# Compressing the keys and values of a sparse-attention layer over 128 partitions instead of twice 64

## The chip, the cores and the metric

One NeuronCore of a Trainium2 chip runs the whole program. The metric is the device time of one execution in microseconds; lower is better. Before the change it is 853.73 us (median of three runs, 852.6 to 855.01). The profile shown below is of one further execution, which took 855.14 us; what the profiler saw of it, the span, is 853.4 us.

## The reference, cut to what matters

The program computes one layer of a hybrid decoder for a prompt of 512 tokens and 8 single-token samples with 256 cached tokens each. One of its four mixers is native sparse attention (NSA). Its compressed branch makes one key and one value for each block of 32 tokens, every 16 tokens, by a linear map of the raw rows of the block (64 numbers a token, for each of 2 heads `kv`):

```python
# phi: (2, 32 * 64, 64), one map for keys (comp 0) and one for values (comp 1)
# raw rows of one sequence: kc_raw, vc_raw of (tokens, 2 heads, 64)
# block n covers tokens 16 n ... 16 n + 31
kc = blocks(kc_raw).reshape(n, 2, 32 * 64) @ phi[0] + phi_b[0]     # then RMS norm
vc = blocks(vc_raw).reshape(n, 2, 32 * 64) @ phi[1] + phi_b[1]
```

A block is two neighbouring chunks of 16 tokens. The kernel therefore multiplies each chunk once by the first half of phi and once by the second, and adds the second product of chunk n+1 to the first product of chunk n. There are 32 chunks of the prompt and 8 times 16 of the samples, 160 in all (`N_CHUNK`).

The rest of the layer matters here only for what stands before and behind: norms and the input projection before, the other mixers, the attention proper, the output projection and a mixture of 32 experts behind.

## The kernel before, in words

All orders are written out by hand: each engine has one block of code, and engines meet at semaphores. PSUM has 8 banks; `psum_jobs()` gives every product a job name and a bank, six of them in rotation. `claim` waits on TensorE until the bank's previous job has been read, `filled` tells the readers, `taken` waits for that, `copied` frees the bank, and `drained` waits until it is free (lines 440 to 456). All matrix data here is fp32. `mm` (line 1110) is a matmul and `turn` (line 1113) a transpose through TensorE, which is why nearly all TensorE rows of the profile name one of these two lines.

The stages that matter, in TensorE's order:

1. Input projection of 5 tiles of tokens (lines 1200 to 1221). Behind the matmuls of each tile TensorE transposes q, k of the tile before (`K` jobs) and its raw compressed rows (`R` jobs). Between the tiles stand the samples: `sample_keys(b)` (line 1182) transposes the cached raw rows of sample b into job `sR{b}` (4 transposes of 128 by 128) and its other keys into `sK{b}` (4 more), and then adds `sample_scores(b - 1)`, two matmuls with 32 output rows. Sample 0 stands in the tile after the first two, 1 and 2 in the next, 3 to 5 in the last, 6 and 7 at the end.
2. Between samples 5 and 6 stands job `RS`, whose product VectorE uses in one long instruction (line 1671) that scales the transposed activations; until that is done the bank of `RS` is not free, and the job that claims it next is `sK7`.
3. The compression (lines 1234 to 1243). ScalarE has copied all `R` and `sR` jobs into `raw`, laid out as partition = 64 kv + d, then component, then token, so one place j of all 160 chunks is every sixteenth number. For each component and each of the 16 places there are two matmuls, kv = 0 on partitions 0 to 63 and kv = 1 on 64 to 127, with 128 output rows (both halves of phi) and 160 columns, each kv into its own bank.
4. ScalarE and VectorE add the two halves (lines 878 to 883 and 1679 to 1685), and TensorE goes on with the other projections in feature-major form (`features`, line 1244), 32 matmuls of 260 columns for each group.

Much later come the attention, the output projection, and then the experts: SyncE's queue loads 32 experts of 6 MB each into three buffers, and the load of expert e starts when TensorE is done with the same part of expert e-3 (lines 580 to 606).

Of the kernel before, what the change touches and what calls it, by code (L numbers as in the profile page):

```python
# [18 lines left out]
ALU = mybir.AluOpType  # L19
ACT = mybir.ActivationFunctionType  # L20
# [3 lines left out]
SEQ = 512  # L24
# [44 lines left out]
def psum_jobs():  # L69

    jobs, turn = [], [0]

    def take(name, bank=None):
        if bank is None:
            bank = turn[0] % 6
            turn[0] += 1
        jobs.append((name, bank))

    def feature(g, halves=(0, 1)):
        for j in halves:  # L80
            take(f"F{g}{j}0")
            take(f"F{g}{j}1")

    take("gain")
    for i in range(4):
        take(f"xTa{i}")
        take(f"xTb{i}")
    take("xT4")
    last = None
    for i in PROJ_TILES:  # L90
        take(f"A{i}")
        if i < 4:
# [12 lines left out]
        last = i  # L105
    take("RS")
    take("K3")
    take("R3")
    for b in SAMPLES_AT["end"]:
        take(f"sR{b}")  # L110
        take(f"sK{b}")
    take("SS", 6)
    take("SW", 7)
    for n in ("CK0", "CK1", "CV0", "CV1"):
        take(n)
# [60 lines left out]
    take("posB")  # L176
    take(f"hTb{others[-1]}")
    take("posC")
    take("cnt", 6)
    return jobs  # L180


def layer_kernel(nc, a, o):
# [7 lines left out]
    with ctx:  # L191
# [45 lines left out]
        ynsa = reg_h.cut(1280, "p (t f) -> p t f", t=5)  # L237
        qT = reg_q.cut(2 * T, "p (g t) -> p g t", g=2)
        kT = reg_q.cut(2 * T, "p (r t) -> p r t", r=2)
        raw = reg_x.t[:, :].rearrange("p (c t) -> p c t", c=2)  # L240
        gain_rows = reg_y.cut(128)[0:KC]
        root_diag = reg_y.cut(512, "p (t n) -> p t n", t=4)
        par_rows = reg_y.cut(128)[0:P_ROWS]
# [5 lines left out]

        phi = reg_a.cut(4096, "p (c j h n) -> p c j h n", c=2, j=16, h=2)
        page_k = [reg_a.cut(768, "p (g f) -> p g f", g=2) for _ in range(PAGE_BUFS // 2)]
        win_k = [reg_a.cut(256, "p (g f) -> p g f", g=2) for _ in range(PAGE_BUFS // 2)]
        vs_cache = reg_a.cut(2048, "p (b g f) -> p b g f", b=NS, g=2)
# [196 lines left out]
        def copied(ins, job):  # L452
            ins.then_inc(bank_read[bank_of[job]], 1)
# [37 lines left out]
        def _(sp_eng):  # L491
# [24 lines left out]
            eng.dma_start(kg[:, :, :], a["nsa_qk_g"].rearrange("l r d -> (l r) d")[2:4].partition_broadcast(128)).then_inc(S["kg_loaded"], 16)  # L516
            eng.dma_start(pages[:, :], a["page_table"].rearrange("b n -> (b n)").unsqueeze(0)).then_inc(S["pages_loaded"], 16)
            for c in range(2):
                for kv in range(2):
                    for half in range(2):  # L520
                        src = a["nsa_phi"].rearrange("l c (h j d) n -> d (l c h) j n", h=2, d=HD)[:, 2 * c + half]
                        eng.dma_start(phi[64 * kv:64 * kv + 64, c, :, kv ^ half, :], src).then_inc(S["phi_loaded"], 16)
            eng.wait_ge(S["blocks_zeroed"], 1)

            for k in range(4):
# [6 lines left out]
            for b in range(NS):  # L532
                k = b % PAGE_BUFS
                if b >= PAGE_BUFS:
                    eng.wait_ge(bank_full[bank_of[f"sK{b - PAGE_BUFS}"]], turn_of[f"sK{b - PAGE_BUFS}"] + 1)
                for g in range(2):
                    page = eng.value_load(pages[0:1, 2 * b + g:2 * b + g + 1], min_val=0, max_val=cache.shape[0] // PAGE - 1)
                    rows_of_page = cache[bass.ds(page * PAGE, PAGE)]
                    eng.dma_start(page_k[k][:, g, :], rows_of_page[:, 0:384]).then_inc(smp_loaded[k], 16)
                    eng.dma_start(vs_cache[:, b, g, :], rows_of_page[:, 384:512]).then_inc(S["vcache_loaded"], 16)  # L540
# [248 lines left out]
        def _(eng):  # L789
# [43 lines left out]
            def feature_qk(i):  # L833

                r, c = ROWS[i], COL[i]
                ps = taken(eng, f"K{i}")
                if i == 4:
                    eng.wait_ge(S["params_made"], 1)
                v = ps[:, 0:4 * r].rearrange("p (g t) -> p g t", g=4)
                eng.activation(qT[:, :, c:c + r], v[:, 0:2, :], ACT.Copy, scale=qg_scaled)  # L840
                copied(copy(kT[:, :, c:c + r], v[:, 2:4, :]), f"K{i}")
                if i < 4:
                    ps = taken(eng, f"R{i}")
                    copied(copy(raw[:, :, c:c + r], ps[:, 0:256].rearrange("p (g t) -> p g t", g=2)), f"R{i}")

            def sample_keys(b):

                ps = taken(eng, f"sR{b}")
                copied(copy(raw[:, :, SEQ + PAST * b:SEQ + PAST * (b + 1)], ps[:, :].rearrange("p (c t) -> p c t", c=2)), f"sR{b}")
                if b >= 2:  # L850
                    eng.wait_ge(S["sample_scores"], b - 1)
                if b == 0:
# [23 lines left out]
                sample_keys(b)  # L876

            for comp, (name, out) in enumerate((("CK", kc_a), ("CV", vcT))):
                for kv in range(2):
                    lo = 64 * kv  # L880
                    other = 64 - lo
                    ps = taken(eng, f"{name}{kv}")
                    eng.activation(out[lo:lo + 64, 0:N_CHUNK - 1], ps[other:other + 64, 1:N_CHUNK], ACT.Identity, bias=params[lo:lo + 64, P_PHI_B + comp:P_PHI_B + comp + 1]).then_inc(S["kc_copied"], 1)
# [224 lines left out]
        def _(eng):  # L1108
# [73 lines left out]
            def sample_keys(b):  # L1182
                eng.wait_ge(smp_loaded[b % PAGE_BUFS], 48 * (b // PAGE_BUFS + 1))
                ps = claim(eng, f"sR{b}")
                for c in range(2):
                    for g in range(2):
                        ins = turn(ps[:, 256 * c + 128 * g:256 * c + 128 * g + 128], page_k[b % PAGE_BUFS][:, g, 128 * c:128 * c + 128])
                filled(ins, f"sR{b}")
                ps = claim(eng, f"sK{b}")
                for g in range(2):  # L1190
# [41 lines left out]
            eng.wait_ge(S["phi_loaded"], 16 * 8)  # L1232
            drained(eng, f"sR{NS - 1}")
            for comp, name in enumerate(("CK", "CV")):
                ps2 = [claim(eng, f"{name}{kv}") for kv in range(2)]
                for j in range(16):
                    for kv in range(2):

                        lo = 64 * kv
                        src = raw[lo:lo + 64, comp, :].rearrange("p (n s) -> p n s", s=16)[:, :, j]  # L1240
                        ins = mm(ps2[kv][:, 0:N_CHUNK], phi[lo:lo + 64, comp, j].rearrange("p h n -> p (h n)"), src, j == 0, j == 15)
                        if j == 15:
                            filled(ins, f"{name}{kv}")
# [326 lines left out]
        def _(eng):  # L1570
# [106 lines left out]
            eng.memset(kcT[:, N_CHUNK - 1:N_CHUNK], 0.0)  # L1677
            eng.memset(vcT[:, N_CHUNK - 1:N_CHUNK], 0.0)
            for comp, (name, first, out) in enumerate((("CK", kc_a, kcT), ("CV", vcT, vcT))):
                for kv in range(2):  # L1680
                    lo = 64 * kv
                    eng.wait_ge(S["kc_copied"], 2 * comp + kv + 1)
                    ps = taken(eng, f"{name}{kv}")
                    copied(tt(out[lo:lo + 64, 0:N_CHUNK - 1], first[lo:lo + 64, 0:N_CHUNK - 1], ps[lo:lo + 64, 0:N_CHUNK - 1], ALU.add), f"{name}{kv}")
                    drained(eng, f"{name}{kv}")
                if comp == 0:
                    eng.sem_inc(S["kc_sum"], 1)
            drained(eng, "CN")
# [473 lines left out]
```

## Time and profile before

| what | value |
|---|---|
| median of 3 runs | 853.73 us |
| profiled execution, its time | 855.14 us |
| profiled execution, its span | 853.4 us |
| TensorE (PE) busy | 730.8 us, 86% |
| VectorE (DVE) busy | 202.8 us, 24% |
| ScalarE (ACT) busy | 148.8 us, 17% |
| GpSimd (POOL) busy | 182.2 us, 21% |
| read from and written to device memory | 264.87 MB |
| compression on TensorE | 95.89 to 113.43 us |

PE stands for matmuls and PEld for the weight loads that run beside them. One fp32 matmul of the code leaves two records of each kind in the trace, a transpose leaves one. A shape such as `64*128 64x160` says 64 rows and 128 columns of weights and a moving operand of 64 partitions by 160 numbers. `SPq` is time in which SyncE issues transfers. A busy time of a merged row overlaps the next row a little, since the end of a matmul record lies behind the start of the next; so lengths are best taken from start to start.

### The profile page before, as it was taken

The page shows a single profiled execution, that of the slowest core. Times are in us where ns is not written, and L with a number is a line of the kernel's source. Part 1 is how long each engine was busy: PE and PEld are TensorE (multiplying, and loading weights), DVE is VectorE, ACT ScalarE, POOL GpSimd, SP SyncE. Part 2 cuts the span into 40 slices and gives each one's busy share as a digit, 9 for nine tenths or more (in the row PEclk, how much of TensorE's full clock was granted, in tenths as well). Part 3 has the DMA queues.
Part 4 walks back from the last instruction along what each step waited for, and adds up shares of the span by engine and source line. Part 5 has one row for each costly group of instructions (what it writes and reads, how often), then busy time and mean ns, then how long its engine had stood idle before and what let it go on. Part 6 is the DMA issues. An engine that isn't in the chain of part 4 may idle for free.

```text
span 853.4 us, 10234 instructions
## 1 busy us (share of the span) xinstructions
PE 730.8 (86%) x3647; PEld 378.4 (44%) x3647; DVE 202.8 (24%) x575; ACT 148.8 (17%) x363; POOL 182.2 (21%) x188
## 2 busy tenths in 40 slices
PE   6999999999989999599999997877777777777783
PEld 5788688777767445333333332222222222222220
DVE  2422303636687112711011100100100100101120
ACT  5223313015544312110100100000000000000000
POOL 5010000061100000113323332132132132132121
PEclk9999999999998999789999999999999999999997
DMA  9652924020800794569999999999999999999992
GB/s 301 121 154 62 278 105 107 2 75 1 296 2 1 282 422 189 198 243 409 410 412 408 408 412 404 418 412 408 413 415 407 415 413 409 416 415 408 416 413 74
DMA packets 76885, 246.52 MB, mean 289 GB/s; under 512 B 24944, under 2 KB 44303, under 8 KB 52235
## 3 DMA queue, kind: packets, MB, share of 16 engines
q1 hardware_dynamic: 63697, 230.96, 68.4%
q0 software_dynamic: 11776, 8.58, 4.6%
q10 hardware_dynamic: 1378, 6.54, 1.9%
q8 instruction: 19, 0.31, 0.1%
q14 instruction: 15, 0.12, 0.0%
HBM read 239.95 MB, written 24.92 MB: 310 GB/s over the span
## 4 chain that ended last, share of the span: by engine, by line
PE 49%; SPq 33%; DMA 6%; DVE 5%; issue 3%; ACT 1%; POOL 1%; ACTq 0%; POOLq 0%; DVEq 0%
PE bank L1110 47%; SPq L588 23%; SPq L595 10%; DMA reg_b<-in_exp_w_gu 3%; PE bank L1113 3%; DMA reg_w<-in_w_in 1%; DMA ffn_in<-reg_x 1%; DVE reg_y L2106 1%; DVE reg_a L1896 1%; ACT reg_y L1093 1%; DVE reg_y L2114 1%; DVE reg_b L1671 1%; DVE small L1856 1%; POOL small L693 0%; DVE reg_y L1903 0%
## 5 line engine op out<-in xcount | busy, mean ns | idle before, releaser
L1110 PE MATMUL bank<-reg_w,reg_y 128*64 128x512 f32 (+2 forms) x512 | 137.0, 573 | 15.6 <-DMA reg_w<-in_exp_w_gu 15.6
L1110 PE MATMUL bank<-reg_a,reg_y 128*64 128x512 f32 x528 | 124.2, 607 | 22.3 <-DMA reg_a<-in_exp_w_gu 16.6
L1110 PE MATMUL bank<-reg_b,reg_y 128*64 128x512 f32 x528 | 122.8, 600 | 22.3 <-DMA reg_b<-in_exp_w_gu 16.6
L2110 DVE TENSOR_TENSOR reg_y<-reg_y,bank 128x256 f32<-128x256 f32 x32 | 13.5, 422 | 418.7 <-ACT reg_y L1093 418.7
L1110 PEld LDWEIGHTS bank<-reg_w,reg_y 128*64 128x64 f32 (+2 forms) x512 | 45.4, 144 | 95.2 <-issue 54.0
L1110 PE MATMUL bank<-reg_b,reg_w 128*128 128x260 f32 x384 | 85.6, 384 | 0.0
L1110 PEld LDWEIGHTS bank<-reg_a,reg_y 128*64 128x64 f32 x528 | 34.6, 138 | 103.3 <-issue 50.5
L1110 PEld LDWEIGHTS bank<-reg_b,reg_y 128*64 128x64 f32 x528 | 34.6, 136 | 101.3 <-issue 58.1
L1110 PEld LDWEIGHTS bank<-reg_b,reg_w 128*128 128x128 f32 x384 | 72.7, 190 | 12.1 <-issue 1.3
L1113 PE MATMUL bank<-small,reg_y 128*128 128x128 f32 (+3 forms) x206 | 42.8, 317 | 24.7 <-DVE reg_y L2110 15.0
L1110 PE MATMUL bank<-reg_w,reg_b 128*128 128x256 f32 (+2 forms) x320 | 62.2, 389 | 1.2 <-DMA reg_w<-in_w_in 1.2
L763 POOL DMA_INDIRECT out_y_p<-reg_y,reg_h x16 | 25.3, 1583 | 168.5 <-ACT reg_y L1097 160.3
L1093 ACT ACTIVATE reg_y<-bank,small 128x256 f32<-128x256 f32 x32 | 15.2, 473 | 264.0 <-PE bank L1110 264.0
L763 POOL DMA_INDIRECT out_y_p<-reg_h x16 | 25.3, 1579 | 160.9 <-issue 160.9
L693 POOL TENSOR_TENSOR small<-small 128x1 f32<-128x1 f32 (+4 forms) x18 | 15.8, 896 | 192.6 <-DVE small L1945 69.8
L1110 PEld LDWEIGHTS bank<-reg_w,reg_b 128*128 128x128 f32 (+1 forms) x320 | 52.1, 174 | 10.0 <-issue 1.3
L1113 PEld LDWEIGHTS bank<-small,reg_y 128*128 128x128 f32 (+3 forms) x206 | 29.6, 202 | 57.4 <-issue 35.4
L1110 PE MATMUL bank<-reg_h,reg_y 128*64 128x512 f32 x160 | 36.6, 600 | 5.2 <-DVE reg_y L2114 5.2
L758 POOL DMA_INDIRECT reg_y<-ffn_in,reg_h x32 | 35.0, 1095 | 21.2 <-issue 19.0
L1113 PE MATMUL bank<-small,reg_b 128*128 128x128 f32 (+2 forms) x133 | 21.3, 284 | 6.8 <-ACT reg_b L976 3.6
L1097 ACT ACTIVATE reg_y<-bank,small 128x512 f32<-128x512 f32 x16 | 11.0, 687 | 87.3 <-PE bank L1110 87.3
L763 POOL DMA_INDIRECT out_y_s<-reg_y,reg_h x16 | 24.9, 1554 | 4.9 <-issue 4.9
(357 smaller groups left out, 632.8 us busy)
## 6 DMA issues: line engine op xcount, KB each, us to landing
reg_a<-in_exp_w_gu SPq DMA_DIRECT2D x44, 1024.0 KB, 27.9
reg_b<-in_exp_w_gu SPq DMA_DIRECT2D x44, 1024.0 KB, 27.6
reg_w<-in_exp_w_gu SPq DMA_DIRECT2D x40, 1024.0 KB, 28.0
reg_a<-in_exp_w_down SPq DMA_DIRECT2D x22, 1024.0 KB, 28.3
reg_b<-in_exp_w_down SPq DMA_DIRECT2D x22, 1024.0 KB, 28.2
reg_h<-in_exp_w_down SPq DMA_DIRECT2D x20, 1024.0 KB, 28.2
reg_w<-in_w_in SPq DMA_DIRECT2D x9, 1024.0 KB, 10.9
reg_w<-in_w_out SPq DMA_DIRECT2D x2, 2048.0 KB, 11.0
```

The costliest lines, as they stand in the source:

```text
L588: eng.dma_start(gu_w[g][:, lo:lo + width, :], src).then_inc(gu_loaded[g][part], 16)
L595: eng.dma_start(down_w[g][:, half], src).then_inc(down_loaded[g][half], 16)
L693: eng.tensor_tensor(out, in_, minus_half[0:out.shape[0], 0:out.shape[-1]], ALU.pow).then_inc(S[s_done], 1)
L758: eng.indirect_dma_start(xe_rows[e % 2], None, x1_dram, idx, bounds_check=2 * T - 1, oob_is_err=False).then_inc(x_gathered[e % 2], 16)
L763: eng.indirect_dma_start(y, idx, y_out[e % 2], None, bounds_check=last, oob_is_err=False, compute_op=ALU.add).then_inc(y_scattered[e % 2], 16)
L1093: eng.activation(silu[b], bank[2 + b][:, 0:256], ACT.Silu, scale=slot_scale[:, 1, bass.ds(e, 1)]).then_inc(S["silu_done"], 1)
L1097: eng.activation(y_out[b], bank[6 + b][:, :], ACT.Copy, scale=slot_scale[:, 0, bass.ds(e, 1)]).then_inc(S["y_copied"], 1)
L1110: return eng.matmul(out, lhsT, rhs, start=start, stop=stop, skip_group_check=True)
L1113: return eng.transpose(out, in_, ident[0:in_.shape[0], 0:in_.shape[0]])
L1671: copied(tt(xnT[:, :, 0:SEQ], xnT[:, :, 0:SEQ], ps[:, :].unsqueeze(1).to_broadcast([128, KC, SEQ]), ALU.mult), "RS")
L1856: eng.tensor_reduce(att_mx[:, col:col + 1], ps[:, 0:width], X_AXIS, ALU.max, negate=True).then_inc(S["att_max"], 1)
L2110: tt(hid[b], silu[b], bank[2 + b][:, 256:512], ALU.mult).then_inc(S["hid_made"], 1)
```

## The change

`raw` is laid out by place within the chunk. A pair of neighbouring tokens lies one above the other: partition = 64 * (token odd) + d, then component, kv, pair j (8 of them), chunk n. With that one place pair of all chunks and both heads is a contiguous piece of 160 numbers for each head, and one matmul over 128 partitions takes 2 times 160 columns. Phi is laid out the same way and takes half the room.

```diff
-        raw = reg_x.t[:, :].rearrange("p (c t) -> p c t", c=2)
+        raw = reg_x.t[:, :].rearrange("p (c k j n) -> p c k j n", c=2, k=2, j=8)
-        phi = reg_a.cut(4096, "p (c j h n) -> p c j h n", c=2, j=16, h=2)
+        phi = reg_a.cut(2048, "p (c j h n) -> p c j h n", c=2, j=8, h=2)
+        reg_a.at = 4096
 # SyncE: phi, 8 transfers of 128 KB in place of 8 of 256 KB
-                        eng.dma_start(phi[64 * kv:64 * kv + 64, c, :, kv ^ half, :], src)
+                        eng.dma_start(phi[64 * odd:64 * odd + 64, c, :, half, :], src)
 # SyncE: a page of 128 tokens onto 64 partitions, two tokens each
-                    eng.dma_start(page_k[k][:, g, :], rows_of_page[:, 0:384])
-                    eng.dma_start(vs_cache[:, b, g, :], rows_of_page[:, 384:512])
+                    pairs = rows_of_page.rearrange("(m o) f -> m o f", o=2)
+                    eng.dma_start(page_k[k][64 * g:64 * g + 64, :, :], pairs[:, :, 0:384])
+                    eng.dma_start(vs_cache[64 * g:64 * g + 64, b, :, :], pairs[:, :, 384:512])
 # ScalarE: job R of a tile, four copies in place of one
-                    copied(copy(raw[:, :, c:c + r], ps[:, 0:256].rearrange("p (g t) -> p g t", g=2)), f"R{i}")
+                    for kv in range(2):
+                        by_pair = ps[64 * kv:64 * kv + 64, 0:256].rearrange("p (c n j o) -> p c n j o", c=2, j=8, o=2)
+                        for odd in range(2):
+                            ins = copy(raw[64 * odd:64 * odd + 64, :, kv, :, c // 16:c // 16 + 8].rearrange("p c j n -> p c n j"), by_pair[:, :, :, :, odd])
+                    copied(ins, f"R{i}")
 # ScalarE: job sR, one copy as before, with a step of 160 numbers in what it writes
-                copied(copy(raw[:, :, SEQ + PAST * b:SEQ + PAST * (b + 1)], ps[:, :].rearrange("p (c t) -> p c t", c=2)), f"sR{b}")
+                copied(copy(raw[:, :, :, :, first:first + N_CMP_S].rearrange("p c k j n -> p (c k) n j"), ps[:, :].rearrange("p (x n j) -> p x n j", x=4, j=8)), f"sR{b}")
 # TensorE: job sR, eight matmuls by the identity in place of four transposes
-                    for g in range(2):
-                        ins = turn(ps[:, 256 * c + 128 * g:256 * c + 128 * g + 128], page_k[b % PAGE_BUFS][:, g, 128 * c:128 * c + 128])
+                    for kv in range(2):
+                        at = 128 * c + 64 * kv
+                        for odd in range(2):
+                            ins = mm(ps[64 * odd:64 * odd + 64, 2 * at:2 * at + 128], page_k[b % PAGE_BUFS][:, odd, at:at + 64], ident, True, True)
 # TensorE: the compression
-                ps2 = [claim(eng, f"{name}{kv}") for kv in range(2)]
-                for j in range(16):
-                    for kv in range(2):
-                        lo = 64 * kv
-                        src = raw[lo:lo + 64, comp, :].rearrange("p (n s) -> p n s", s=16)[:, :, j]
-                        ins = mm(ps2[kv][:, 0:N_CHUNK], phi[lo:lo + 64, comp, j].rearrange("p h n -> p (h n)"), src, j == 0, j == 15)
+                ps = claim(eng, name)
+                for j in range(8):
+                    ins = mm(ps[:, 0:2 * N_CHUNK].rearrange("p (k n) -> p k n", k=2), phi[:, comp, j].rearrange("p h n -> p (h n)"), raw[:, comp, :, j, :], j == 0, j == 7)
+                filled(ins, name)
 # the jobs CK0, CK1, CV0, CV1 (four banks) become CK and CV (two banks); ScalarE and VectorE
 # read the same four pieces of 64 x 159 numbers as before, from two banks
```

Two places of TensorE's order show the change. The first is sample 1, behind the projection of its tile (the third of five); `bank` is PSUM, `small` holds the identity, `reg_a` and `reg_b` hold the cached rows, `reg_h` the rows of the prompt. Before:

```order
L1110 MATMUL bank<-reg_w,reg_b 128x268 x8
L1113 MATMUL bank<-small,reg_b 128x128 x2
L1113 MATMUL bank<-small,reg_h 128x128 x4
L1113 MATMUL bank<-small,reg_a 128x128 x8
L1110 MATMUL bank<-reg_a,reg_b 32x257 x2
```

and now:

```order
L1118 MATMUL bank<-reg_w,reg_b 128x268 x8
L1121 MATMUL bank<-small,reg_b 128x128 x2
L1121 MATMUL bank<-small,reg_h 128x128 x4
L1118 MATMUL bank<-small,reg_a 64x128 x8
L1121 MATMUL bank<-small,reg_a 128x128 x4
L1118 MATMUL bank<-reg_a,reg_b 32x257 x2
```

Of the eight transposes of a sample four remain; the other four have become eight matmuls with 64 output rows, and TensorE goes through one more kind of output shape per sample. The second place is the end of the samples and the compression (`reg_x` is `raw`). Before:

```order
L1113 MATMUL bank<-small,reg_b 128x128 x8
L1110 MATMUL bank<-reg_a,reg_b 32x257 x4
L1110 MATMUL bank<-reg_x,reg_a 128x160 x64
L1110 MATMUL bank<-reg_b,reg_w 128x260 x32
L1110 MATMUL bank<-reg_b,small 128x160
```

and now:

```order
L1118 MATMUL bank<-small,reg_b 64x128 x8
L1121 MATMUL bank<-small,reg_b 128x128 x4
L1118 MATMUL bank<-reg_a,reg_b 32x257 x4
L1118 MATMUL bank<-reg_x,reg_a 128x320 x16
L1118 MATMUL bank<-reg_b,reg_w 128x260 x32
L1118 MATMUL bank<-reg_b,small 128x160
```

The 64 matmuls of 160 columns have become 16 of 320; what stands behind them is the same.

## Rows read from the trace of the kernel before

**Rows 1.** The page's chain of work that ended last, by engine.

```profile
PE 49%; SPq 33%; DMA 6%; DVE 5%; issue 3%; ACT 1%; POOL 1%; ACTq 0%; POOLq 0%; DVEq 0%
```

**Rows 2.** Stretches: length, busy time per engine, clock, DMA share, GB/s.

```profile
365.00:503.00 138.00, 128.07 (x588) 46.76 (x586) 16.14 (x34) 13.36 (x22) 43.22 (x31) 0.98 0.98 389
503.00:833.00 330.00, 261.83 (x1132) 80.21 (x1131) 32.49 (x72) 23.90 (x41) 86.37 (x61) 1.00 1.02 412
```

**Rows 3.** SyncE in order of time: start, length, what; first load into a used buffer.

```profile
370.13 5.47 SPq L588 DMA_DIRECT2D reg_a<-in_exp_w_gu  x4
```

**Rows 4.** TensorE in order of time: the compression and the first features.

```profile
95.89 17.61 PE L1110 MATMUL bank<-reg_x,reg_a 64*128 64x160 f32 x128
113.43 14.29 PE L1110 MATMUL bank<-reg_b,reg_w 128*128 128x260 f32 x64
```

**Rows 5.** TensorE in order of time, samples 1 and 2.

```profile
65.79 1.04 PE L1113 MATMUL bank<-small,reg_a 128*128 128x128 f32 x8
66.75 0.63 PE L1110 MATMUL bank<-reg_a,reg_b 128*32 128x257 f32 x4
67.31 1.09 PE L1113 MATMUL bank<-small,reg_b 128*128 128x128 f32 x8
68.33 0.63 PE L1110 MATMUL bank<-reg_a,reg_b 128*32 128x257 f32 x4
```

**Rows 6.** TensorE in order of time, RS to the last sample.

```profile
88.31 1.16 PE L1110 MATMUL bank<-reg_y,small 128*128 128x128 f32 x8
89.31 0.38 PE L1113 MATMUL bank<-small,reg_b 128*128 128x128 f32 x2
...
91.49 0.66 PE L1113 MATMUL bank<-small,reg_b 128*128 128x128 f32 x4
93.99 0.66 PE L1113 MATMUL bank<-small,reg_b 128*128 128x128 f32 x4 [1.84 <-DVE reg_b L1671]
94.58 1.38 PE L1110 MATMUL bank<-reg_a,reg_b 128*32 128x257 f32 x8
```

**Rows 7.** VectorE in order of time: the scaling that reads RS.

```profile
89.51 4.42 DVE L1671 TENSOR_TENSOR reg_b<-reg_b,bank 128x4096 f32<-128x4096 f32 x1 [0.69 <-PE bank L1110]
```

**Rows 8.** TensorE, matmuls with few output rows, at three places.

```profile
30.16 3.80 PE L1110 MATMUL bank<-reg_w,reg_b 128*8 128x256 f32 x64
...
161.39 3.61 PE L1110 MATMUL bank<-reg_a,reg_b 128*32 128x128 f32 x64 [1.63 <-DVE reg_b L1765]
164.93 0.41 PE L1110 MATMUL bank<-reg_h,reg_b 8*32 8x128 f32 x4
...
380.63 7.04 PE L1110 MATMUL bank<-reg_b,reg_y 128*64 128x512 f32 x32
```

**Rows 9.** TensorE, attention scores over 64 partitions, 256 and 384 columns.

```profile
222.48 0.70 PE L1110 MATMUL bank<-reg_q 64*128 64x256 f32 x4
223.12 0.29 PE L1110 MATMUL bank<-causal_bf,ident_bf 128*128 128x128 bf16 x2
...
236.46 0.92 PE L1110 MATMUL bank<-reg_q 64*128 64x384 f32 x4
237.31 0.29 PE L1110 MATMUL bank<-causal_bf,ident_bf 128*128 128x128 bf16 x2
```

**Rows 10.** ScalarE in order of time, copies of jobs K2, R2 and sR4.

```profile
84.05 0.39 ACT L792 ACTIVATE reg_q<-bank 128x256 f32<-128x256 f32 x1
84.31 0.89 ACT L792 ACTIVATE reg_x<-bank 128x256 f32<-128x256 f32 x2
...
85.84 0.60 ACT L792 ACTIVATE reg_x<-bank 128x512 f32<-128x512 f32 x1
86.34 0.20 ACT L792 ACTIVATE reg_a<-reg_q 128x2 f32<-128x2 f32 x1
```

**Rows 11.** SyncE's queue: the loads of weights for the features.

```profile
89.68 52.74 SPq L550 DMA_DIRECT2D reg_w<-in_w_in  x6
```

**Rows 12.** Stretches: length, clock, DMA share, GB/s.

```profile
104.00:106.00 2.00, 1.00 0.98 307
106.00:108.00 2.00, 1.00 0.06 20
```

More of the change, by code:

```diff
@@ L113, in psum_jobs @@
     take("SW", 7)
-    for n in ("CK0", "CK1", "CV0", "CV1"):
-        take(n)
+    take("CK")
+    take("CV")
     feature("U")
@@ L518, in _ @@
             for c in range(2):
-                for kv in range(2):
+                for odd in range(2):
                     for half in range(2):
-                        src = a["nsa_phi"].rearrange("l c (h j d) n -> d (l c h) j n", h=2, d=HD)[:, 2 * c + half]
-                        eng.dma_start(phi[64 * kv:64 * kv + 64, c, :, kv ^ half, :], src).then_inc(S["phi_loaded"], 16)
+                        src = a["nsa_phi"][0, c].rearrange("(h j o d) n -> h o d j n", h=2, o=2, d=HD)[half, odd]
+                        eng.dma_start(phi[64 * odd:64 * odd + 64, c, :, half, :], src).then_inc(S["phi_loaded"], 16)
             eng.wait_ge(S["blocks_zeroed"], 1)
@@ L538, in _ @@
                     rows_of_page = cache[bass.ds(page * PAGE, PAGE)]
-                    eng.dma_start(page_k[k][:, g, :], rows_of_page[:, 0:384]).then_inc(smp_loaded[k], 16)
-                    eng.dma_start(vs_cache[:, b, g, :], rows_of_page[:, 384:512]).then_inc(S["vcache_loaded"], 16)
+                    pairs = rows_of_page.rearrange("(m o) f -> m o f", o=2)
+                    eng.dma_start(page_k[k][64 * g:64 * g + 64, :, :], pairs[:, :, 0:384]).then_inc(smp_loaded[k], 16)
+                    eng.dma_start(vs_cache[64 * g:64 * g + 64, b, :, :], pairs[:, :, 384:512]).then_inc(S["vcache_loaded"], 16)
                 eng.dma_start(win_k[k][:, :, :], win_state[b].rearrange("(g p) f -> p g f", p=128)[:, :, 0:128]).then_inc(smp_loaded[k], 16)
@@ L843, in feature_qk @@
                     ps = taken(eng, f"R{i}")
-                    copied(copy(raw[:, :, c:c + r], ps[:, 0:256].rearrange("p (g t) -> p g t", g=2)), f"R{i}")
+                    for kv in range(2):
[3 more added lines that the diff above has]
+                    copied(ins, f"R{i}")
             def sample_keys(b):
                 ps = taken(eng, f"sR{b}")
-                copied(copy(raw[:, :, SEQ + PAST * b:SEQ + PAST * (b + 1)], ps[:, :].rearrange("p (c t) -> p c t", c=2)), f"sR{b}")
+                first = N_CMP_P + N_CMP_S * b
+                copied(copy(raw[:, :, :, :, first:first + N_CMP_S].rearrange("p c k j n -> p (c k) n j"), ps[:, :].rearrange("p (x n j) -> p x n j", x=4, j=8)), f"sR{b}")
                 if b >= 2:
@@ L878, in _ @@
             for comp, (name, out) in enumerate((("CK", kc_a), ("CV", vcT))):
+                ps = taken(eng, name)
                 for kv in range(2):
@@ L881, in _ @@
                     other = 64 - lo
-                    ps = taken(eng, f"{name}{kv}")
-                    eng.activation(out[lo:lo + 64, 0:N_CHUNK - 1], ps[other:other + 64, 1:N_CHUNK], ACT.Identity, bias=params[lo:lo + 64, P_PHI_B + comp:P_PHI_B + comp + 1]).then_inc(S["kc_copied"], 1)
+                    first = N_CHUNK * kv + 1 - kv
+                    eng.activation(out[lo:lo + 64, 0:N_CHUNK - 1], ps[other:other + 64, first:first + N_CHUNK - 1], ACT.Identity, bias=params[lo:lo + 64, P_PHI_B + comp:P_PHI_B + comp + 1]).then_inc(S["kc_copied"], 1)
             eng.wait_ge(S["kc_sum"], 1)
@@ L1185, in sample_keys @@
                 for c in range(2):
-                    for g in range(2):
-                        ins = turn(ps[:, 256 * c + 128 * g:256 * c + 128 * g + 128], page_k[b % PAGE_BUFS][:, g, 128 * c:128 * c + 128])
+                    for kv in range(2):
+                        at = 128 * c + 64 * kv
+                        for odd in range(2):
+                            ins = mm(ps[64 * odd:64 * odd + 64, 2 * at:2 * at + 128], page_k[b % PAGE_BUFS][:, odd, at:at + 64], ident, True, True)
                 filled(ins, f"sR{b}")
@@ L1234, in _ @@
             for comp, name in enumerate(("CK", "CV")):
-                ps2 = [claim(eng, f"{name}{kv}") for kv in range(2)]
-                for j in range(16):
-                    for kv in range(2):
-                        lo = 64 * kv
-                        src = raw[lo:lo + 64, comp, :].rearrange("p (n s) -> p n s", s=16)[:, :, j]
-                        ins = mm(ps2[kv][:, 0:N_CHUNK], phi[lo:lo + 64, comp, j].rearrange("p h n -> p (h n)"), src, j == 0, j == 15)
-                        if j == 15:
-                            filled(ins, f"{name}{kv}")
+                ps = claim(eng, name)
+                for j in range(8):
+                    ins = mm(ps[:, 0:2 * N_CHUNK].rearrange("p (k n) -> p k n", k=2), phi[:, comp, j].rearrange("p h n -> p (h n)"), raw[:, comp, :, j, :], j == 0, j == 7)
+                filled(ins, name)
             def features(g, halves_of=(0, 1)):
@@ L1679, in _ @@
             for comp, (name, first, out) in enumerate((("CK", kc_a, kcT), ("CV", vcT, vcT))):
+                eng.wait_ge(S["kc_copied"], 2 * comp + 2)
+                ps = taken(eng, name)
                 for kv in range(2):
[L1681 to L1685, printed above, removed]
+                    lo, at = 64 * kv, (N_CHUNK + 1) * kv
+                    ins = tt(out[lo:lo + 64, 0:N_CHUNK - 1], first[lo:lo + 64, 0:N_CHUNK - 1], ps[lo:lo + 64, at:at + N_CHUNK - 1], ALU.add)
+                copied(ins, name)
+                drained(eng, name)
                 if comp == 0:
```

## The prediction, on record before the result

> **What bounds the kernel now.** I read the chain of waits first: TensorE holds 49% of it and SyncE's issuing 33% [rows 1]. So there are two regimes, and the stretches show where they meet [rows 2]: from 365 to 503 us TensorE is busy 128 of 138 us, from 503 to 833 us only 262 of 330 while the DMA engines are full at 412 GB/s. A change at 30 to 113 us can move the end only if the DMA-bound part starts earlier with it. It does: the first load into a buffer that was already used starts at 370.13 us, when TensorE has finished that part of the first expert [rows 3], and the chain in front of it is TensorE nearly throughout. So I carry one microsecond of TensorE's path before 113 us to the end as one microsecond. A cold clock at the first expert can add or take about a microsecond of that at random.
>
> Second, TensorE in order of time around the edit. The compression runs from 95.89 to 113.43 us, 17.54 us, with no idle time before or behind it [rows 4]. The samples are 1.52 us each (65.79 to 67.31 us) with no idle time either [rows 5]. Only at the end does TensorE wait: 1.84 us before the last four transposes [rows 6], for the VectorE instruction that starts when RS is filled and lasts 4.42 us [rows 7].
>
> **The compression: what it costs and why.** 64 pairs of records in 17.54 us are 0.274 us a pair. Are the two members of a pair, on partitions 0 to 63 and 64 to 127, really serial? The attention scores use the same two halves with contiguous operands: four records of 256 columns take 0.64 us to the next kind, four of 384 take 0.85 [rows 9]. 128 more columns cost 0.21 us for four records; that is two rounds of 0.107, so the two halves run side by side, at 0.83 ns a column. In the compression a pair of 160 columns at this rate would be 0.133 us. It is twice that. What differs is the operand: every sixteenth number. So I read the half rate as the price of the step, and the merging of the two halves as worth nothing in itself.
>
> The Trainium skill says the same of both: in "TensorE: Matmul & The Clock Gate", part 3, matmuls on different row groups run concurrently, and "SBUF — State Buffer", in the section on door 1, says that accesses which cross to a new 16-byte line each time pay a penalty. By the first rule alone a change from 64 to 128 partitions saves nothing; by the second the contiguous layout is what saves. The trace agrees with the first (0.21 us above) and is consistent with the second (0.274 against 0.133 us).
>
> After: 16 matmuls are 32 records of 320 contiguous columns. The features give the price, 14.29 us for 64 records of 260 columns [rows 4], 0.223 us or 0.858 ns a column; 320 columns are 0.275 us and 32 of them 8.8 us. Saved: 17.54 - 8.8 = 8.7 us, and one change of tile shape (64 to 128 rows) at its exit, 0.15 us by the price below. Together -8.9 us. Bounds: at 0.83 ns a column 8.5 us are left (-9.2); if columns of `raw` kept today's 1.71 ns, 17.5 us (no gain).
>
> **The samples: what is added on TensorE.** Four transposes of each sR become eight matmuls, 16 records, that alternate between output rows 0 to 63 and 64 to 127. Prices from rows: eight transposes take 0.96 us before a new shape when they follow other transposes and 1.02 when they follow a different shape [rows 5]; four take 0.59 (93.99 to 94.58) [rows 6]. So a transpose is 0.108 us and a change of shape 0.09 + 0.06 = 0.15 us.
>
> The alternating pair isn't in the trace at 128 columns. Lower bound: with 8 output rows, four column groups and 256 columns, 64 records take 3.80 us, 0.238 a round of four [rows 8], and experts' pairs of 64 output rows take 7.04 us for 32 records of 512 columns, 0.44 a pair [rows 8]. A quarter of that is 0.11 us for a pair of 128 columns. Upper bound: four groups of 32 output rows at 128 columns take 161.39 to 164.93 us for 64 records, 0.22 a round [rows 8], twice the streaming time of 0.107; so a round with many short loads can cost double. I take 0.112, since this row has four weight loads a round and the new code two, and the experts' row has the same tile shape.
>
> A sample then adds 8 x 0.112 - 4 x 0.108 + 0.15 (a second change of shape) = 0.62 us. Samples 0, 1, 3 and 6 follow transposes, where no change of shape was needed before: 0.15 more each. On the path, samples 0 to 5: 6 x 0.62 + 3 x 0.15 = 4.2 us. Upper bound, with 0.22: 8 x 0.22 - 0.43 + 0.15 = 1.48, so 9.3 us; lower, with the changes of shape hidden, 6 x 0.45 = 2.7 us.
>
> "TensorEngine Tiling (Array Packing)" of the Trainium skill says in its key properties that changing the tiling mode drains the engine, and in its gotchas that column tiling excludes the fp32 transpose mode, which is why matmuls stand here. It speaks against this change; the trace shows the drain at 0.15 us.
>
> Samples 6 and 7 add 2 x 0.62 + 0.15 = 1.4 us between RS and sK7. There TensorE waits 1.84 us for VectorE, whose 4.42 us run from RS and not from the samples. The addition disappears in the wait: cost 0, and 1.3 us with the upper bound (3.1 - 1.84).
>
> **What lies beside.** ScalarE: each R job becomes four copies. A copy of 256 columns starts 0.26 us after the one before it and one of 512 takes 0.50 [rows 10], so four of 128 are some 0.6 to 0.7 us, 0.4 more, in front of the copies of the samples. TensorE needs a sample's sK copy one sample later (now 2.1 us), and ScalarE's work for one is 0.50 + 0.10 + 0.50 = 1.1 us. This covers the four copies, and a strided write of sR up to three times as slow (1.5 + 0.1 + 0.5 = 2.1). Cost 0; at four times as slow about 3.5 us, 3.0 of it the two copies of sR6 and sR7 at 2.0 in place of 0.5 us in front of the last scores. Phi's loads halve, in front of the pages, which can only arrive earlier: 0. The feature weights are issued from 89.68 us [rows 11], behind page loads that wait for sK3, and all four land by 106 us [rows 12]. Both move: sK3 is filled about 2.9 us later, so the last lands near 109 us, and the first of the four, the only one needed then, well before; the features start at 95.89 + 4.2 + 8.8 = 108.9 us. ScalarE and VectorE read CK and CV from two banks, 14 us ahead of the product that needs them: 0.
>
> **The sum.** -8.9 + 4.2 + 0 = -4.7 us. The profiled execution took 855.14 us (span 853.4), so the changed kernel under the same conditions takes 850.4; the median of before is 853.73, 1.4 lower, and from it I get 849.0 us.
>
> **The rivals.**
> 1. Double rounds: the pairs of sR cost 0.22 us, as the row with 32 output rows does. For it: that row is the only one with 128 columns in column groups. Against it: it has twice the groups. Then +9.3 + 1.3 - 8.9 = +1.7 us, 855.4.
> 2. Slower: the alternating output halves don't overlap and each weight load is exposed. 16 records of 0.108 + 0.06 us are 2.7 us in place of 0.43, and with the change of shape 2.4 us a sample: 6 x 2.4 + 0.45 = 14.9, samples 6 and 7 exceed the wait by 3.1, so -8.9 + 18.0 = +9.1 us, 862.8. Against it stands the experts' pair. It breaks even at a round of 0.19 us and is slower by over 2.6 us from 0.23 on.
> 3. The change doesn't do what it says: the half rate is not the step's but the operand's or the tile's, and 320 columns cost 0.55 us. Then no gain, +4.2 us, 857.9. The features and the experts read at full rate from the same kind of memory, against it.
> 4. ScalarE's strided writes are four times as slow: -4.7 + 3.5, 852.5.
>
> **How the numbers follow.** Forecast (a round up to 0.14 us) 65%, 849.0 with its own range 846.8 to 851; rival 1 and rounds between 17%; rival 2 7%; rival 3 4%; rival 4 or another partial loss 7%. A difference under 0.3%, 2.6 us, can't be told from none. The low end is the lower bound of the samples, -6.2, and a run 0.7 below it: 846.8. The high end reaches into rival 1 until a fifth at most is left out: 854.2. Faster 0.69, same 0.21, slower 0.10.
>
> **What would show it.** In the changed profile: 32 records of 128x320 in 8.8 us; each sR 16 records in 0.9 to 1.0 us (1.8 with rival 1, 2.7 with rival 2); the wait of 1.84 us before the last transposes down to about 0.4; features from 109 us; the first reused expert buffer loaded from about 365.5 us. I am wrong if the 16 records of an sR take more than 1.5 us, if the 320 columns take more than 0.4 us, or if a wait for a DMA stands in front of the features.

## The result and the profile after

The changed kernel takes 846.41 us (median of five runs, 844.2 to 848.26) against 854.07 us in the same comparison (five runs, 852.6 to 855.01): a ratio of 0.9908 with the interval 0.9889 to 0.9926, 7.7 us less. The forecast was 849.0 us, and the low end of its range, 846.8 us, lies 0.4 us above the result. Comparisons leave out the few runs that were disturbed.

The profiled execution took 846.41 us, span 844.7. These are the page's rows for the engines' busy times and, further down, for the chain by engine, of the changed kernel:

```profile
PE 723.8 (86%) x3647; PEld 372.5 (44%) x3647; DVE 202.8 (24%) x575; ACT 156.4 (19%) x375; POOL 182.3 (22%) x188
...
PE 43%; SPq 33%; DMA 13%; DVE 4%; issue 3%; ACT 2%; POOL 1%; ACTq 0%; POOLq 0%; DVEq 0%
```

ScalarE has grown by 7.6 us of busy time (148.8 before). The change of regime is where it was in the work, and starts earlier on the clock: SyncE's first load into a used expert buffer stands at 361.58 us, against 370.13 [rows 3].

```profile
361.58 5.47 SPq L590 DMA_DIRECT2D reg_a<-in_exp_w_gu  x4
```

That is 8.55 us earlier, and the span is 8.7 us shorter. The carry from the front of the kernel to its end holds. Now TensorE in order of time in the changed kernel (start, length, engine, line, tiles, count, idle time before and its releaser): the tile 0 projection, samples 1 and 2, the end of the samples, the compression and the first features.

```profile
13.32 14.21 PE L1118 MATMUL bank<-reg_w,reg_b 128*128 128x256 f32 x64 [1.17 <-DMA reg_w<-in_w_in]
27.47 1.02 PE L1121 MATMUL bank<-small,reg_y 46*128 46x46 f32 x5
...
64.72 1.09 PE L1118 MATMUL bank<-small,reg_a 128*64 128x128 f32 x16
65.75 0.65 PE L1121 MATMUL bank<-small,reg_a 128*128 128x128 f32 x4
66.33 0.63 PE L1118 MATMUL bank<-reg_a,reg_b 128*32 128x257 f32 x4
66.89 1.09 PE L1118 MATMUL bank<-small,reg_b 128*64 128x128 f32 x16
...
96.07 0.66 PE L1121 MATMUL bank<-small,reg_b 128*128 128x128 f32 x4 [0.66 <-DVE reg_b L1677]
96.65 0.63 PE L1118 MATMUL bank<-reg_a,reg_b 128*32 128x257 f32 x4
97.66 0.63 PE L1118 MATMUL bank<-reg_a,reg_b 128*32 128x257 f32 x4 [0.38 <-ACT reg_a L794]
98.22 8.88 PE L1118 MATMUL bank<-reg_x,reg_a 128*128 128x320 f32 x32
106.93 14.19 PE L1118 MATMUL bank<-reg_b,reg_w 128*128 128x260 f32 x64
```

The samples and the compression are what the prediction said. A sample takes 2.17 us (64.72 to 66.89), the 16 records of its sR 1.03 us of it; the compression takes 106.93 - 98.22 = 8.71 us in place of 17.54 [rows 4]. From tile 0's end to the features are 106.93 - 27.47 = 79.46 us; in the kernel before, with its own row below, 113.43 - 29.21 = 84.22 us. So the edit is worth 4.76 us, and -4.7 was forecast. The same stretch takes 79.45 us (27.36 to 106.81) and 79.46 us (26.71 to 106.17) in the two later profiles of the changed kernel.

Most of the rest, 3.4 us, does not lie at the edit but in TensorE's clock at two other places. First tile 0's projection in the kernel before, then the granted clock of the two places there (stretch, length, PE busy, clock, DMA share, GB/s):

```profile
13.38 15.90 PE L1110 MATMUL bank<-reg_w,reg_b 128*128 128x256 f32 x64 [1.21 <-DMA reg_w<-in_w_in]
29.21 1.02 PE L1113 MATMUL bank<-small,reg_y 46*128 46x46 f32 x5
```

```profile
15.00:18.00 3.00, 3.00 (x9) 0.50 1.10 348
162.00:164.00 2.00, 2.00 (x48) 0.50 0.00 0
```

Tile 0's 64 records take 15.83 us before and 14.15 us after, with the same instructions: the clock was granted at 0.50 (1.2 in place of 2.4 GHz) in the one and at full speed in the other, 1.7 us. The second place is the product with 32 output rows, 3.54 us before [rows 8]. In the changed kernel, product and clock are:

```profile
154.71 1.95 PE L1118 MATMUL bank<-reg_a,reg_b 128*32 128x128 f32 x64 [1.55 <-DVE reg_b L1772]
156.59 0.41 PE L1118 MATMUL bank<-reg_h,reg_b 8*32 8x128 f32 x4
```

```profile
155.00:156.00 1.00, 1.00 (x48) 1.00 0.00 0
```

1.88 us, again 1.7 us less. So -4.76 - 1.68 - 1.66 = -8.1 of the 8.7 us are accounted for. Of the other 0.6 us, 0.45 lie in front of the first reused expert buffer (8.55 us) and 0.15 behind it; their cause stays open.

These short stretches of half clock are not the only ones. Both profiles also have a longer one in the attention and one where the first expert starts. Here is the one in the attention, before and in the changed kernel:

```profile
253.60:260.40 6.80, 6.80 (x30) 0.50 0.00 0
245.00:251.80 6.80, 6.79 (x28) 0.50 0.00 0
```

### The profile page after: what moved, and what is told of

Read it like the earlier page. It is cut to its first block, busy times and chain, and to the rows that moved or that the text cites. A ratio compares the mean times of both kernels' runs of the same rounds, so it can differ in the third digit from the quotient of the medians.

```text
span 844.7 us, 10242 instructions
## 1 busy us (share of the span) xinstructions
PE 723.8 (86%) x3647; PEld 372.5 (44%) x3647; DVE 202.8 (24%) x575; ACT 156.4 (19%) x375; POOL 182.3 (22%) x188
## 4 chain that ended last, share of the span: by engine, by line
PE 43%; SPq 33%; DMA 13%; DVE 4%; issue 3%; ACT 2%; POOL 1%; ACTq 0%; POOLq 0%; DVEq 0%
PE bank L1118 41%; SPq L590 23%; SPq L597 10%; DMA reg_b<-in_exp_w_gu 6%; DMA reg_a<-in_exp_w_gu 3%; PE bank L1121 2%; DMA reg_w<-in_w_in 1%; DMA ffn_in<-reg_x 1%; DVE reg_a L1903 1%; DVE reg_y L2113 1%; DVE small L1863 1%; ACT reg_y L1101 1%; DVE reg_y L2121 0%; POOL small L695 0%; DVE reg_y L1910 0%
## 5 line engine op out<-in xcount | busy, mean ns | idle before, releaser
L1118 PE MATMUL bank<-reg_w,reg_b 128*128 128x256 f32 (+2 forms) x320 | 60.5, 383 | 1.2 <-DMA reg_w<-in_w_in 1.2
L1105 ACT ACTIVATE reg_h<-bank,small 128x512 f32<-128x512 f32 x16 | 11.0, 687 | 85.3 <-PE bank L1118 85.3
```

The costliest lines, as they stand in the source:

```text
L1105: eng.activation(y_out[b], bank[6 + b][:, :], ACT.Copy, scale=slot_scale[:, 0, bass.ds(e, 1)]).then_inc(S["y_copied"], 1)
L1118: return eng.matmul(out, lhsT, rhs, start=start, stop=stop, skip_group_check=True)
```

## The experiments

Ten runs were made, in three batches, each beside runs of the kernel before. A ratio here is the comparison's own estimate with its 95% interval; it is not always the quotient of the two medians.

**Is the surplus in the clock?** The changed kernel and the kernel before ran again without an edit.

> The changed kernel once more. Theory 1: the edit is worth the 4.8 us that TensorE's path shows between the start of the second projection tile and the features (+4.1 us of samples, -8.8 us of compression); the rest of the measured 7.7 us is two cold-clock stretches (1.7 us in the first projection tile, 1.7 us in the samples' values product) that this profile did not have and that fall where they will. Then about 849 us against 854, and its profile may be cold at either place. Theory 2: the change itself keeps the clock up, and the gain is again 7 to 8 us, 846 us, with both places warm.

Measured: 847.32 us (844.84 to 849.24) against 853.39; ratio 0.9943 (0.9924 to 0.9962), 4.9 us by the ratio, while the two medians are 6.1 us apart.

> The kernel before once more, as a measure of noise. Theory 1: the same 854 us within 1.5 us on the median, but its profile has the cold stretches at 14 to 18 us and 161 to 165 us only sometimes. Theory 2: cold at 161 to 165 us again, since what stands in front of it is the same.

Measured: 853.22 us, ratio 1.0004 (0.999 to 1.0019). Its profile has tile 0 and the product at full speed and the clock low at other places, one of them a block of features:

```profile
13.00 14.21 PE L1110 MATMUL bank<-reg_w,reg_b 128*128 128x256 f32 x64 [0.84 <-DMA reg_w<-in_w_in]
...
143.40 15.98 PE L1110 MATMUL bank<-reg_b,reg_w 128*128 128x260 f32 x64
...
161.64 1.96 PE L1110 MATMUL bank<-reg_a,reg_b 128*32 128x128 f32 x64 [1.63 <-DVE reg_b L1765]
163.52 0.41 PE L1110 MATMUL bank<-reg_h,reg_b 8*32 8x128 f32 x4
```

```profile
144.00:147.00 3.00, 3.00 (x8) 0.50 0.99 198
```

The other one is at 93 us, in front of the compression. In the last batch the changed kernel ran a third time.

> The changed kernel once more, on another set of runs. Theory: the change itself is worth what the trace shows at the edit, 8.8 us saved in the compression and about 4.1 us spent in the samples, 4.7 to 5.2 us in all; what the first comparison showed beyond it (7.7 us) is where the cold clock stretches fell in those runs. So 4 to 6.5 us below the kernel before, and at an equal mean granted clock 5.2 us below it (over the runs so far: 847.0 against 852.2 us at 0.980). Rival: the change also takes about 2 us from somewhere else (its shorter row of small matmuls, or fewer cold stretches because of it): then 7 to 8 us again, and also at an equal clock over 6 us.

Measured: ratio 0.9914 (0.9889 to 0.9939), 7.3 us by the ratio; the median of the five runs compared is 847.1 us against 853.4, 6.3 us. This profile has the clock low in the product with 32 output rows, 153.94 to 157.44 us:

```profile
153.94 3.57 PE L1118 MATMUL bank<-reg_a,reg_b 128*32 128x128 f32 x64 [1.54 <-DVE reg_b L1772]
```

```profile
155.00:157.00 2.00, 2.00 (x44) 0.50 0.00 0
```

So either kernel has the product at either clock: 1.9 and 3.5 us in both. The clock of this product is not tied to the change, and three comparisons of the same two kernels gave 7.7, 4.9 and 7.3 us. What the clock does to a run can be taken out in good part, since each run has its mean granted clock. A straight line of time over clock, with one slope for all kernels, through the 97 compared runs whose clock is listed (of the batches, and the first five of the changed kernel), has a slope of 4.5 us for 0.01 of the clock and these values at a clock of 0.980 (standard error in brackets):

| kernel | runs | mean us | mean clock | us at 0.980 |
|---|---|---|---|---|
| before | 53 | 853.2 | 0.9782 | 852.4 (0.2) |
| changed | 16 | 846.9 | 0.9803 | 847.0 (0.3) |
| samples alone | 8 | 856.7 | 0.9792 | 856.3 (0.4) |
| changed, with transposes | 6 | 847.3 | 0.9773 | 846.1 (0.4) |
| layout alone | 10 | 844.2 | 0.9789 | 843.7 (0.3) |
| contiguous read | 4 | 843.6 | 0.9810 | 844.1 (0.5) |

At an equal clock the change is worth 5.4 us, plus or minus 0.6. The correction is rough: the mean counts a stretch of half clock wherever it falls, also where the first expert starts and TensorE was busy for 6.94 of 17.00 us (352.6 to 369.6 us of the kernel before). Both expectations for the third run are met in part: 7.3 us as the rival had it, but under 6 at an equal clock as the theory had it. The changed kernel's mean clock is 0.002 higher, another 1.0 us. Whether that is chance or comes with the change stays open, and so does the 0.6 us between 5.4 and the 4.76 us that the traces show at the edit.

**The samples alone.** The kernel before, with each sR by matmuls with 64 output rows:

```
-  ins = turn(ps[:, 256*c + 128*g : ... + 128], page_k[...][:, g, 128*c : 128*c + 128])
+  for kv in range(2):
+      ins = mm(ps[64*kv:64*kv + 64, 256*c + 128*g : ... + 128],
+               page_k[...][:, g, 128*c + 64*kv : ... + 64], ident, True, True)
```

> The kernel before with only the four transposes of each sR replaced by eight matmuls by the identity with 64 output rows. By the prediction: 1.09 us in place of 0.5 for each, +0.62 us a sample for samples 0 to 5 and 0.15 for three changes of shape, +4.2 us; samples 6 and 7 disappear in the wait for VectorE. 858.2 us. By theory 2 the matmuls may also change the clock behind them.

Measured: 857.05 us (854.8 to 858.1), ratio 1.0044 (1.0027 to 1.0061), 3.7 us slower, and 4.0 at an equal clock (standard error 0.4). Its rows on TensorE:

```profile
65.91 1.09 PE L1110 MATMUL bank<-small,reg_a 128*64 128x128 f32 x16
66.94 0.66 PE L1113 MATMUL bank<-small,reg_a 128*128 128x128 f32 x4
67.52 0.63 PE L1110 MATMUL bank<-reg_a,reg_b 128*32 128x257 f32 x4
68.08 1.09 PE L1110 MATMUL bank<-small,reg_b 128*64 128x128 f32 x16
...
97.25 0.66 PE L1113 MATMUL bank<-small,reg_b 128*128 128x128 f32 x4 [0.66 <-DVE reg_b L1672]
97.84 1.38 PE L1110 MATMUL bank<-reg_a,reg_b 128*32 128x257 f32 x8
99.15 17.61 PE L1110 MATMUL bank<-reg_x,reg_a 64*128 64x160 f32 x128
```

2.17 us a sample, the wait down from 1.84 to 0.66 us, the compression as before. From tile 1's matmuls to the compression are 63.89 us (35.26 to 99.15) against 60.08 before, 3.8 us. The term of +4.2 us stands by itself, a little too large, and so does the cover of samples 6 and 7.

**The layout alone.** The kernel before with the rows of `raw` laid out by place in the chunk, written so by ScalarE, read with 160 neighbours at a time; the 64 matmuls over 64 partitions and the transposes stay:

```
-raw = reg_x.t[:, :].rearrange("p (c t) -> p c t", c=2)
+raw = reg_x.t[:, :].rearrange("p (c j n) -> p c j n", c=2, j=16)
-copy(raw[:, :, c:c + r], ...)
+copy(raw[:, :, :, c//16:c//16 + 8].rearrange("p c j n -> p c n j"), ...)   # sR alike
-src = raw[lo:lo + 64, comp, :].rearrange("p (n s) -> p n s", s=16)[:, :, j]
+src = raw[lo:lo + 64, comp, j, :]
```

> The kernel before with raw laid out by place (component, place of 16, chunk) and nothing else: still 64 matmuls over 2 x 64 partitions, transposes for the samples, phi as before; ScalarE writes with a step. If the half rate of the compression is the price of the step: pairs of 160 columns in 0.137 us, compression 8.8 us in place of 17.5, samples 1.5 us each as before, sum -8.7 us, 845.3 us by theory 1, and better than the changed kernel by 4 us. If it is the price of two 64-row halves: the compression stays at 17.5 us and the time at 854.

Measured: 842.87 us, the median of the four runs compared (842.07 to 845.9), ratio 0.9898 (0.9872 to 0.9923). It ran again:

> The kernel before with the rows of raw laid out by place in the chunk, and nothing else: 64 matmuls over 64 partitions and the transposes stay. Theory: the layout alone carries the whole gain (8.7 us in the compression) and the matmuls of the samples cost the changed kernel 4.1 us of it; less about 0.4 us of waits for ScalarE. So 8.2 us below the kernel before, about 844.5 us, and 3 us below the changed kernel in the same batch. Rival: its low time in the first batch (844.7 us with four undisturbed runs) was luck with the clock: then about 847, as the changed kernel.

Measured: 844.67 us (842.46 to 846.88), ratio 0.9893 (0.9868 to 0.9919). At an equal clock it is 8.7 us below the kernel before and 3.3 us below the changed one. TensorE in its first profile:

```profile
65.53 1.09 PE L1114 MATMUL bank<-small,reg_b 128*128 128x128 f32 x8
66.74 0.63 PE L1111 MATMUL bank<-reg_a,reg_b 128*32 128x257 f32 x4
...
94.48 8.96 PE L1111 MATMUL bank<-reg_x,reg_a 64*128 64x160 f32 x128
103.37 8.81 PE L1111 MATMUL bank<-reg_b,reg_w 128*128 128x260 f32 x39
```

The compression takes 8.89 us with all of its 128 records over 64 partitions: 0.139 us a pair in place of 0.274. Merging the halves is worth 8.89 - 8.71 = 0.18 us; the prediction had 0.15 us for the change of shape at its exit, and no run separates the merging from that. So the gain is the layout's, and the part that costs 4 us (the matmuls of sR, which put odd tokens on the upper partitions) buys only the 0.18 us. This version beats both kernels.

**Is it the step itself, and which steps?** Three kernels change nothing but where a matmul reads, so their compressed keys and values are made from the wrong tokens, with as many matmuls and columns. The first reads contiguously from the old layout.

```
+src = raw[lo:lo + 64, comp, 160*j:160*j + 160]
```

> The kernel before, with one slice changed: each matmul of the compression reads 160 neighbouring numbers of raw in place of every sixteenth. The values are therefore wrong; nothing else moves, ScalarE's copies are as before. If the step costs the half rate: 64 pairs in 0.137 us, 8.8 us, and the time 8.7 us down, 844.7. If two 64-row halves are the cost: 17.5 us as before. Against the layout-only kernel it shows what ScalarE's stepped writes cost: under 0.5 us.

Measured: 843.94 us, ratio 0.9884 (0.9859 to 0.9909). Its compression, and the clock in two parts of it:

```profile
95.61 10.22 PE L1110 MATMUL bank<-reg_x,reg_a 64*128 64x160 f32 x128
105.76 14.29 PE L1110 MATMUL bank<-reg_b,reg_w 128*128 128x260 f32 x64
```

```profile
95.70:98.10 2.40, 2.40 (x18) 0.50 1.10 348
98.30:105.50 7.20, 7.20 (x110) 1.00 1.06 333
```

10.15 us, of which the stretch at half the clock costs about 1.3 (2.6 us from 95.61 to 98.2, half of it lost), so 8.85 at full speed: the layout's 8.89. ScalarE's writes are as in the kernel before here, so nothing but the read explains the gain. The second kernel reads every second number for the keys and every fourth for the values.

```
+step = (2, 4)[comp]
+src = raw[lo:lo + 64, comp, 160*(j % 8) : 160*(j % 8) + 160*step : step]
```

> The kernel before, with the compression reading every second number for the keys and every fourth for the values (wrong values, same count of columns). A graded cost: if crossing a 16-byte line at each number is what costs, a step of 2 (8 bytes) runs at or near the full rate, 0.137 us a pair, and a step of 4 (16 bytes) at the half rate, 0.27. If any step costs: both 0.27. If only long steps cost: both 0.137.

Measured: 849.61 us in one run. Three microseconds out of each half, both at full clock:

```profile
97.00:100.00 3.00, 3.00 (x48) 1.00 1.10 349
102.00:105.00 3.00, 3.00 (x24) 1.00 0.77 242
```

48 records against 24. A count in a window is coarse; from start to start, a pair of records takes 0.142 us at step 2 and 0.283 at step 4, against 0.136 contiguous (layout alone) and 0.271 at step 16. So step 2 runs within 5% of the contiguous rate, and step 4 (16 bytes) costs as much as step 16 (64 bytes), within 5% again. The Trainium skill says in "SBUF — State Buffer", in the section on door 1, that a 16-byte line needs at least two accesses for full bandwidth. The trace agrees at both sides: two numbers of a line are read at step 2, one at step 4. The third is the changed kernel reading every eighth number of its rows, 320 columns over 128 partitions:

```
+raw[:, comp].rearrange("p k j n -> p k (j n)").rearrange("p k (n j) -> p k n j", j=8)[:, :, :, j]
```

> The changed kernel, 16 matmuls over 128 partitions and 320 columns, but reading every eighth number of raw in place of neighbouring ones (wrong values). If the step costs and the merging is worth nothing: 32 records of 0.54 us, 17.3 us, no gain left in the compression, and the whole slower than before by the 4 us of the samples, 857.5. If merging is what helped: 8.8 us.

Measured: 856.32 us in one run.

```profile
98.02 18.65 PE L1118 MATMUL bank<-reg_x,reg_a 128*128 128x320 f32 x32
116.49 5.88 PE L1118 MATMUL bank<-reg_b,reg_w 128*128 128x260 f32 x26
```

18.47 us, 1.80 ns a column against 0.85. Over 128 partitions the step halves the rate as it does over 64, and the merging saves nothing of it; rival 3 had about this price (0.55 us for 320 columns, 0.58 here) on the wrong cause.

**The transposes back in the changed kernel.** Four transposes for each sR, and all else as changed.

```
-for kv in range(2): ... for odd in range(2): ins = mm(ps[64*odd:64*odd + 64, ...], ..., ident, True, True)
+for g in range(2): ins = turn(ps[:, 256*c + 128*g : ... + 128], page_k[...][:, g, 128*c : 128*c + 128])
```

> The changed kernel with the four transposes of each sR put back in place of the eight matmuls; the rows of raw then come from the wrong tokens, so its compressed values of the samples are not the reference's. The prediction's terms: -4.2 us against the changed kernel (0.62 us a sample for six samples, 0.15 for three changes of shape), minus what the stepped ScalarE copy costs at the last sample. About 844.5 us, as the kernel with only the layout changed (844.7).

Measured: 847.3 us (845.48 to 849.07), ratio 0.9934 (0.9913 to 0.9954): no faster than the changed kernel's 847.32 and 847.1 us in the other two batches, and 0.9 us at an equal clock (standard errors 0.3 and 0.4), where about 3 were expected. A miss. TensorE and ScalarE show why:

```profile
66.97 1.09 PE L1121 MATMUL bank<-small,reg_b 128*128 128x128 f32 x8
69.29 0.63 PE L1118 MATMUL bank<-reg_a,reg_b 128*32 128x257 f32 x4 [1.23 <-ACT reg_a L794]
...
88.44 0.63 PE L1118 MATMUL bank<-reg_a,reg_b 128*32 128x257 f32 x4 [1.24 <-ACT reg_a L794]
```

```profile
85.01 0.39 ACT L794 ACTIVATE reg_q<-bank 128x256 f32<-128x256 f32 x1
85.28 2.65 ACT L794 ACTIVATE reg_x<-bank 64x128 f32<-64x128 f32 x5
87.72 0.20 ACT L794 ACTIVATE reg_a<-reg_q 128x2 f32<-128x2 f32 x1
87.79 0.59 ACT L794 ACTIVATE reg_a<-bank 128x512 f32<-128x512 f32 x1
88.27 1.09 ACT L794 ACTIVATE reg_x<-bank 128x512 f32<-128x512 f32 x1
```

ScalarE needs 2.65 us for the four copies of R2 and the first copy of an sR; in the kernel before these are two copies in 0.89 us [rows 10]. The sR copy starts at 86.89 us:

```profile
86.89 1.03 ACT L794 ACTIVATE reg_x<-bank 128x512 f32<-128x512 f32 x1
```

So the four R copies alone take 1.61 us, where the one copy of before took 0.27 us (84.31 to 84.58). With the short samples TensorE reaches the scores behind the second sample of a tile before ScalarE has copied their keys, and waits 1.23 and 1.24 us. In the changed kernel the longer samples hide this, and in the layout alone, with one R copy, 0.2 us of each is left (the second sample's transposes and the scores behind them start at 65.53 and 66.74 us). From the start of tile 1's matmuls at 35 us to the compression the changed kernel takes 64.15 us (34.07 to 98.22), this one 62.90 (35.47 to 98.37).

## Why the prediction was wrong

The direction was right and the terms on TensorE's path were near; the time lies 0.4 us outside the range. The step that failed is the last one, from the sum to a time and a range, which left too little room for TensorE's clock.

- **The compression**: 8.8 us forecast, 8.71 measured; the cause, the step of the operand and not the halves, is shown by the layout alone, the contiguous read and the steps 2 and 4. Rival 3 is out.
- **The samples**: 2.14 us each forecast (1.52 + 0.62), 2.17 measured; +4.2 us as a sum, 64.15 - 60.08 = 4.07 in the profiles (35.81 to 95.89 before), 3.8 us in the profile of the kernel with nothing else changed and 4.0 in its times. The pair of 128 columns costs about 0.12 us with its change of shape left out. Rivals 1 and 2 are out.
- **The wait**: 1.84 us was to go to about 0.4; it went to 0.66, and a new wait of 0.38 us for ScalarE stands behind it, in front of the last scores. The sum is as forecast, but one step is not: ScalarE's cost was not covered to the last, since the copy of sR7 is stepped too. In the samples alone, where it is not, the wait of 0.66 us is there and the one of 0.38 is not. One such copy takes 0.86 us to the next instruction against 0.50. Rival 4 had a factor of 4; it is 1.7. The four R copies were put at 0.6 to 0.7 us and take 1.6; that stayed hidden only behind the longer samples, which is part luck.
- **What failed** is the step that carries the sum to a time and a range: "A cold clock at the first expert can add or take about a microsecond", and the low end as "the lower bound of the samples, -6.2, and a run 0.7 below it". Both put the clock at one place and at about one microsecond. There it is about right: in two profiles of the changed kernel the way from the features to the first reused expert buffer takes 254.65 and 253.25 us, with the clock low for 17.0 and for 13.7 us of it where the expert starts. What was left out are the short stretches of half clock elsewhere. The profile before had two of them ahead of the experts, which cost 1.7 us each; the changed kernel's first profile had none of these, and its third had one. Over the runs the clock's mean moves between 0.973 and 0.984, at 4.5 us for 0.01. The distance from 849.0 us to the changed kernel's mean of 846.9 is made up of 0.5 us in the base (three runs gave 853.73, 53 runs give 853.2), 1.0 us of clock, and 0.7 us by which the change at an equal clock (5.4, plus or minus 0.6) exceeds 4.7. The last is just above its error, and the profiles, with 4.76 us at the edit each time, do not show where it would lie. The first comparison's median is 0.5 us lower still. A range of plus and minus 3 us around the forecast would have been honest with three runs to start from.
- **A row misread**: the upper bound of the samples and rival 1, 17 in 100, rested on the product at 161.39 us taking 0.22 us a round. That row ran at half the clock. At full speed it is 1.88 us for 16 rounds, 0.117 us. A window over this row of the profile before gives the clock, 0.50, and the prediction had not looked. With it, rival 1 had nothing to stand on, and one of the two clock stretches would have been seen ahead of the result.

What stays open: why the changed kernel's clock was a little higher on average; the 0.6 us between the accounted 8.1 and the 8.7 us of the two profiled spans; and the 0.6 us between 4.76 at the edit and 5.4 at an equal clock.

## What to carry to other kernels

An fp32 operand that TensorE reads at a step of 4, 8 or 16 numbers costs double here; lay it out in the order of reading, and let the engine that copies it out of PSUM pay for the step, but look whether that copy is on the path. Try the layout apart from whatever else it seemed to suggest: here the merging of the halves gave 0.18 us and cost 4. Before a row serves as a bound, read its granted clock; and when a difference of a few microseconds matters, compare runs at an equal clock, since three comparisons of the same two kernels put them 4.9, 7.3 and 7.7 us apart.

## What the runs showed of the hardware

- The price of the step is close to a switch: a pair of records of 160 columns takes 0.142 us at step 2 and 0.283 at step 4, against 0.136 contiguous and 0.271 at step 16; at step 8 a column takes 1.80 ns against 0.85 contiguous. It is the same over 64 and over 128 partitions.
- Two matmuls of 160 columns on the two halves of the partitions run at the rate of one of 320 over all: 8.89 and 8.71 us for the same work.
- ScalarE pays less for a stepped write than TensorE for a stepped read: 0.86 us in place of 0.50 for 512 numbers a partition. Four copies of 64x128 took 1.6 us, where one of 128x256 took 0.27.
- Short stretches at a clock of 0.50 came at different places from one execution to the next of the same kernel, with TensorE busy throughout in those shown (3.00 of 3.00 us, 2.00 of 2.00), and cost up to 1.7 us each. Longer ones came in the attention and at the start of the first expert in the profiles of both kernels.
